# Modulation of the mixers: shift weights as halves, two tiles of activations each turn, first pieces of the recurrence split within the last turn

## The reference, cut to what matters

```python
s_lat, s_ctx = silu(c), silu(c_ctx)
m_lat = split(s_lat @ w_mod + b_mod, 6); m_ctx = split(s_ctx @ w_mod + b_mod, 6)
hx = rmsnorm(x, norm_mix) * (1 + m_lat[1]) + m_lat[0]
hc = rmsnorm(ctx, norm_mix) * (1 + m_ctx[1]) + m_ctx[0]
... = split_cols(hx @ w_in); ... = split_cols(hc @ w_in)
```

## Time and profile before

| | us |
|---|---|
| median of 3 runs | 3080.35 |
| profiled execution, its own time | 3083.66 |
| its span | 3081.8 |
| first product of the modulation starts | 13.22 |
| transposes of the tokens | 72.51 to 81.15 |
| last row of the modulation copied | 136.64 |
| first pieces of the recurrence | 147.86 to 172.42 |
| mean granted TensorE clock | 0.947 of full |

### The profile page before, as it was taken

How to read it: one execution, slowest core, us unless ns; L and a number is a source line. 1 busy time by engine, 2 the same in 40 slices (tenths; PEclk the granted TensorE clock), 3 DMA queues, 4 the chain that set the end, 5 groups by cost and what they waited for, 6 DMA issues and landing times.

```text
span 3081.8 us, 31629 instructions
## 1 busy us (share of the span) xinstructions
PE 2660.0 (86%) x11041; PEld 1807.1 (59%) x11041; DVE 1930.2 (63%) x2622; ACT 912.0 (30%) x1241; POOL 599.6 (19%) x580
## 2 busy tenths in 40 slices
PE   7899997999999999999999855969778876868777
PEld 3488875878776889998877723334333432323233
DVE  2389997443565868887555746555555665566645
ACT  1167775432544433333434100101111111101100
POOL 0000000000000000000000244434344434343333
PEclk9999998999999999999999977989989998989999
DMA  8633333542323968887555789999999999999998
GB/s 334 221 127 115 122 108 125 190 179 96 137 96 125 366 266 341 337 336 286 205 217 212 287 344 378 418 421 407 421 407 421 402 421 411 421 396 422 422 422 356
DMA packets 126508, 902.85 MB, mean 293 GB/s; under 512 B 14016, under 2 KB 15552, under 8 KB 17216
## 3 DMA queue, kind: packets, MB, share of 16 engines
q0 software_dynamic: 82944, 604.02, 47.7%
q1 hardware_dynamic: 38736, 278.94, 24.3%
q10 hardware_dynamic: 4720, 18.57, 1.6%
HBM read 899.33 MB, written 2.13 MB: 293 GB/s over the span
## 4 chain that ended last, share of the span: by engine, by line
PE 44%; DMA 29%; DVE 12%; issue 9%; ACT 3%; POOL 1%; DVEq 0%; ACTq 0%; POOLq 0%
DMA u<-in_peer_u,idx 27%; PE ps L445 9%; PE ps L488 7%; PE ps L490 7%; PE ps L489 7%; PE ps L765 5%; PE ps L503 3%; DVE u L1670 2%; DMA v<-in_peer_v,idx 2%; DVE wl L1148 2%; POOL v L1765 1%; PE ps L460 1%; ACT wh L827 1%; DVE ub L1232 1%; PE ps L642 1%
## 5 line engine op out<-in xcount | busy, mean ns | idle before, releaser
L765 PE MATMUL ps<-v,dg 128*128 128x512 f32 x1920 | 882.2, 616 | 188.5 <-DMA v<-in_peer_v,idx 92.7
L1670 DVE SCALAR_TENSOR_TENSOR u<-u,hN 128x2048 f32<-128x2048 f32 x256 | 586.5, 2292 | 495.8 <-DMA u<-in_peer_u,idx 484.4
L1148 DVE TENSOR_TENSOR wl<-w,wh 128x1024 fp32r<-128x1024 f32 x432 | 524.6, 1222 | 407.5 <-ACT wh L827 406.5
L765 PEld LDWEIGHTS ps<-v,dg 128*128 128x128 f32 x1920 | 370.7, 197 | 695.9 <-issue 538.0
L827 ACT ACTIVATE wh<-w 128x1024 fp32r<-128x1024 f32 x432 | 453.5, 1058 | 679.1 <-PE ps L490 411.8
L1755 POOL DMA_INDIRECT u<-in_peer_u,idx x256 | 270.1, 1055 | 856.0 <-DVE u L1670 447.5
L445 PE MATMUL ps<-both,wh 128*128 128x256 f32 x2048 | 372.4, 285 | 5.3 <-DVE y L1360 5.1
L1100 ACT ACTIVATE dg<-con,wt 128x128 f32<-128x128 f32 x240 | 93.0, 399 | 835.4 <-PE ps L765 830.2
L1765 POOL DMA_INDIRECT v<-in_peer_v,idx x256 | 295.3, 1154 | 198.0 <-PE ps L765 111.5
L445 PEld LDWEIGHTS ps<-both,wh 128*128 128x128 f32 x2048 | 321.0, 193 | 10.2 <-issue 9.0
L1747 POOL DMA_DIRECT2D mr<-in_wmod x64 | 34.0, 532 | 1397.7 <-DVE br_lo L1488 980.0
(11 more groups left out here) (240 smaller groups left out, 2807.3 us busy)
## 6 DMA issues: line engine op xcount, KB each, us to landing
w<-in_stream SPq DMA_DIRECT2D x260, 1024.0 KB, 4.8
mr<-in_wmod POOLq DMA_DIRECT2D x64, 1024.0 KB, 7.0
wg<-in_gates ACTq DMA_DIRECT2D x8, 512.0 KB, 3.4
wx<-in_stream SPq DMA_DIRECT2D x4, 1024.0 KB, 8.0
u<-in_peer_u,idx POOLq DMA_INDIRECT x256, 16.7
v<-in_peer_v,idx POOLq DMA_INDIRECT x256, 18.0
xs<-in_ctx ACTq DMA_DIRECT2D x1, 2048.0 KB, 17.3
xs<-in_x ACTq DMA_DIRECT2D x1, 2048.0 KB, 23.2
```

The lines of the kernel that those rows point to most:

```text
L765: last = mm(ps[:, b, :], dg[:, k % 4, :], V[n % NV][:, b * 512:(b + 1) * 512], start=(k == 0), stop=(k == TOPK - 1))
L1148: tt(wl[p % SPLITS][:, :, :], W[s][:, q * PIECE:(q + 1) * PIECE, :], wh[p % SPLITS][:, :, :].bitcast(F32), ALU.subtract)\
L1670: stt(U[n % NU][:, :], U[n % NU][:, :], 1.0, hN[:, t, :], ALU.mult, ALU.mult, accum_out=dot[:, t, k:k + 1])\
```

## The change: what it does

The rows of the shift and of the scale of the same 256 columns are made in one turn; there are eight turns c, and the stream is ordered so that each brings two halves of shift weights (`W[0]`, `W[1]`) and two of scale weights (`W[2]`, `W[3]`). The scale stays in f32. The shift weights are parted into `wh` and `wl` by ScalarE and VectorE, piece by piece, and multiplied in fp32r: `wh` against four columns (`sS`, the high and the low part of `sT`) and `wl` against two. After each turn its rows are copied, transposed (`rows_turn`) and made into columns (`mod_cols`) for two tiles. From turn 4 on, tiles are modulated inside the turns, two or four in each, the context side by ScalarE and the latent side by VectorE. The tokens' squares, their scaling and the copies of their transposes are shared out between ScalarE and VectorE, and between the splits; their DMAs are issued behind the first four splits. The tokens are transposed after turn 3. The first weight pieces of the recurrence are parted around the end of turn 7. Not shown: the new places of the small buffers, the lists of steps.

```diff
+        sS = sb("sS", R_S + 192, [P, KT, 4], F32R)
+        mrow = sb("mrow", R_S + 1216, [P, 2, 2 * CW])
...
+        MODS, MP = MOD_H // 4, 4
+        FREED = (3, 4, 7, 8)
+        mod_hi, mod_lo = sem("mod_hi"), sem("mod_lo")
+        xt_copied = [sem("xt_dve"), sem("xt_act")]
+        rows_copied, rows_turned = sem("rows_copied"), sem("rows_turned")
+        VM = Steps(sem("dve_mod"), ["b0", "b1", "s0", "s1"])
+        AH = Steps(sem("act_h"), ["vc", "hc", "hx"])
+        VV = Steps(sem("dve_v"), ["x"])
+        VH = Steps(sem("dve_h"), [f"lo_{w}" for w in "cx"])
+        SIDES = (("c", hc, 0, 1), ("x", hx, T, 0))
...
-            by_pe(1, LRU0 // RING + 1)
+            for i in range(1, LRU0 // RING + 1):
+                for s in (2, 0, 3, 1):
+                    if s < 2:
+                        sp.wait_ge(mod_lo, MP * (i - 1) + 2 * (s + 1))
+                    else:
+                        sp.wait_ge(piece_used, 8 * (i - 1) + 4 * s - 6)
+                    sp.dma_start(W[s][:, :, :], a_stream[i * RING + s].rearrange("p (k n) -> p k n", n=CW)).then_inc(arrived[s], 16)
...
+            def mod_turn(c):
+                b = 2 * (c % 2)
+                if c >= 2:
+                    pe.wait_ge(rows_copied, 2 * (c - 1))
+                for h_ in (0, 1):
+                    pe.wait_ge(arrived[2 + h_], 16 * (c + 1))
+                    for kk in range(HK):
+                        last = mm(ps[0:2, b + 1, 0:CW], sT[:, h_ * HK + kk, :], W[2 + h_][:, kk, :], start=(h_ == 0 and kk == 0),
+                                  stop=(h_ == 1 and kk == HK - 1), skip_group_check=True)
+                    last.then_inc(piece_used, 2)
+                    for p in (2 * h_, 2 * h_ + 1):
+                        m = MP * c + p
+                        pe.wait_ge(mod_lo, m + 1)
+                        for kk in range(PIECE):
+                            k = p * PIECE + kk
+                            mm(ps[0:4, b, 0:CW], sS[:, k, 0:4], wh[m % SPLITS][:, kk, :], start=(k == 0), stop=False, skip_group_check=True)
+                            last = mm(ps[0:2, b, 0:CW], sS[:, k, 0:2], wl[m % SPLITS][:, kk, :], start=False,
+                                      stop=(k == KT - 1), skip_group_check=True)
+                        last.then_inc(piece_used, 1)
+                    if h_ == 0 and c >= 4:
+                        rows_turn(c - 1)
+            def rows_turn(c):
+                pe.wait_ge(rows_copied, 2 * (c + 1))
+                if c:
+                    pe.wait_ge(*VM.at(c - 1, "s0"))
+                for i in range(2):
+                    nc.tensor.transpose(ps[:, 4, 4 * i:4 * i + 4], mrow[0:4, c % 2, i * P:(i + 1) * P], ident[0:4, 0:4])
+                for i in range(2):
+                    last = nc.tensor.transpose(ps[:, 4, 8 + 2 * i:10 + 2 * i], mrow[0:2, c % 2, CW + i * P:CW + (i + 1) * P], ident[0:2, 0:2])
+                last.then_inc(rows_turned, 1)
+            def first_piece(p):
+                pe.wait_ge(*VH.at((p + 1) * PIECE - 1, "lo_x"))
+                proj_both(LRU0, 0, 0, 0, part=(p,))
+            pe.wait_ge(*V0_.at(0, "sl"))
+            for c in range(2):
+                mod_turn(c)
             pe.wait_ge(par_in, 32)
+            rows_turn(0)
+            mod_turn(2)
+            rows_turn(1)
+            mod_turn(3)
             for k in range(KT):
                 if k == 0:
+                    pe.wait_ge(*VM.at(1, "s0"))
+                    pe.wait_ge(*A0.at(0, "xn1"))
                     pe.wait_ge(*V0_.at(0, "xn3"))
                 if k >= 4:
-                    pe.wait_ge(*V0_.at(0, f"xT{k - 4}"))
+                    pe.wait_ge(xt_copied[k % 2], (k - 4) // 2 + 1)
                 for t in range(4):
                     last = nc.tensor.transpose(ps[:, 4 + k % 4, t * P:(t + 1) * P], xs[:, t, k * P:(k + 1) * P], ident)
                 last.then_inc(*P0.inc(f"xT{k}"))
-            mod_turns(MOD_H // 8, MOD_H // 4)
-            pe.wait_ge(*VM.at(MOD_H // 4 - 1, "m1"))
+            pe.wait_ge(xt_copied[0], KT // 2)
+            rows_turn(2)
+            for c in range(4, MODS):
+                mod_turn(c)
+            first_piece(0)
+            rows_turn(MODS - 1)
+            for p in range(1, 4):
+                first_piece(p)
...
+            act.wait_ge(par_in, 32)
+            fn(sig0[:, :], pc("c", 0, 2 * KT), ACT.Sigmoid).then_inc(*A0.inc("sig"))
+            def mod_split(m):
+                c, p = divmod(m, MP)
+                act.wait_ge(arrived[p // 2], 16 * (c + 1))
+                if c:
+                    act.wait_ge(piece_used, 8 * (c - 1) + FREED[p])
+                fn(wh[m % SPLITS][:, :, :], W[p // 2][:, p % 2 * PIECE:(p % 2 + 1) * PIECE, :], ACT.Copy).then_inc(mod_hi, 1)
+            def tiles(c):
+                act.wait_ge(*VM.at(c, "s1"))
+                for k in (2 * c, 2 * c + 1):
+                    for w, to, at, v in SIDES:
+                        x, scale, bias = xT[:, k, at:at + T], mcol[:, KT + k, v:v + 1], mcol[:, k, v:v + 1]
+                        if w == "c":
+                            fn(x, x, ACT.Identity, scale=scale, bias=bias).then_inc(*AH.inc("vc"))
+                            act.wait_ge(*AH.at(k, "vc"))
+                        else:
+                            act.wait_ge(*VV.at(k, "x"))
+                        fn(to[0][:, k, :], x, ACT.Copy).then_inc(*AH.inc("h" + w))
+            for m in range(4):
+                mod_split(m)
             act.dma_start(xs[:, 0:2, :], a_ctx.rearrange("(t p) d -> p t d", p=P)).then_inc(xs_in, 16)
             act.dma_start(xs[:, 2:4, :], a_x.rearrange("(t p) d -> p t d", p=P)).then_inc(xs_in, 16)
-            act.wait_ge(par_in, 32)
-            fn(sig0[:, :], pc("c", 0, 2 * KT), ACT.Sigmoid).then_inc(*A0.inc("sig"))
             act.wait_ge(*V0_.at(0, "abs"))
             fn(lm[2][:, :], lm[1][:, :], ACT.Exp, scale=-1.0).then_inc(*A0.inc("ez"))
+            for m in range(4, 8):
+                mod_split(m)
             act.wait_ge(xs_in, 32)
             for i in range(4):
                 if i:
                     act.wait_ge(*A0.at(0, f"ss{i - 1}"))
                 fn(junk[:, :], xs[:, i, :], ACT.Square, accum_out=ssq[:, i:i + 1]).then_inc(*A0.inc(f"ss{i}"))
+                mod_split(8 + i)
             act.wait_ge(*A0.at(0, "ss3"))
             act.wait_ge(*V0_.at(0, "eps"))
             fn(rin0[:, :], ssq[:, :], ACT.Sqrt, scale=1.0 / D, bias=tiny[:, 1:2]).then_inc(*A0.inc("rt"))
+            mod_split(12)
+            act.wait_ge(*V0_.at(0, "rin"))
+            for i in (0, 1):
+                fn(xs[:, i, :], xs[:, i, :], ACT.Copy, scale=rin0[:, i:i + 1]).then_inc(*A0.inc(f"xn{i}"))
+                mod_split(13 + i)
+            mod_split(15)
+            for k in range(1, KT, 2):
+                act.wait_ge(*P0.at(0, f"xT{k}"))
+                fn(xT[:, k, :], ps[:, 4 + k % 4, :], ACT.Copy).then_inc(xt_copied[1], 1)
             def split(first, turn, per, p, slots=None):
@@ -827,12 +903,17 @@
                 fn(wh[p % SPLITS][:, :, :], W[s][:, q * PIECE:(q + 1) * PIECE, :], ACT.Copy).then_inc(hi_done, 1)
-            for k in range(KT):
-                for w, to, at in (("c", hc, 0), ("x", hx, T)):
-                    act.wait_ge(*VH.at(0, f"{w}{k}"))
-                    if k % PIECE == 0 and w == "c":
-                        split(LRU0, 0, 0, k // PIECE)
-                    fn(to[0][:, k, :], xT[:, k, at:at + T], ACT.Copy).then_inc(*AH.inc(f"{w}{k}"))
+            for c in range(4, MODS):
+                for p in range(4):
+                    mod_split(MP * c + p)
+                for i in {4: (0, 1), 5: (2, 3), 6: (4, 5)}.get(c, ()):
+                    tiles(i)
+            split(LRU0, 0, 0, 0)
+            split(LRU0, 0, 0, 1)
+            tiles(MODS - 2)
+            split(LRU0, 0, 0, 2)
+            tiles(MODS - 1)
+            split(LRU0, 0, 0, 3)
...
+            dve.wait_ge(*V0_.at(0, "st"))
+            def mod_low(m):
+                c, p = divmod(m, MP)
+                dve.wait_ge(mod_hi, m + 1)
+                tt(wl[m % SPLITS][:, :, :], W[p // 2][:, p % 2 * PIECE:(p % 2 + 1) * PIECE, :], wh[m % SPLITS][:, :, :].bitcast(F32), ALU.subtract)\
+                    .then_inc(mod_lo, 1)
+            def mod_rows(c):
+                if c >= 2:
+                    dve.wait_ge(rows_turned, c - 1)
+                dve.wait_ge(piece_used, 8 * c + 8)
+                nc.vector.tensor_copy(mrow[0:4, c % 2, 0:CW], ps[0:4, 2 * (c % 2), 0:CW]).then_inc(rows_copied, 1)
+                nc.vector.tensor_copy(mrow[0:2, c % 2, CW:2 * CW], ps[0:2, 2 * (c % 2) + 1, 0:CW]).then_inc(rows_copied, 1)
+            def mod_cols(c):
+                dve.wait_ge(rows_turned, c + 1)
+                got = ps[:, 4, 0:8].rearrange("p (b v) -> p b v", v=4)
+                shift, scale = mcol[:, 2 * c:2 * c + 2, :], mcol[:, KT + 2 * c:KT + 2 * c + 2, :]
+                wide_ = lambda x: x.unsqueeze(2).to_broadcast([P, 2, 2])
```

(94 more changed lines are left out.)

18 lines of the change are left out of this document (1 added, 17 removed).

## The result

The changed kernel takes 3053.2 us, the median of 4 runs (3051.26 to 3056.05), beside 3080.83 (3078.01 to 3081.86) of the kernel before. The ratio is 0.9913, with an interval of 0.9895 to 0.9930: 27 us, or 0.9%, faster. The forecast was 3052. Its range of 3040 to 3066 holds the time.

A forecast was written before the change was run, and what follows sets the result against it. TensorE, busy 2660.0 of 3081.8 us, and a serial joint were to bound the first stage. fp32r 24.6, joint some 16, transposes 1.5, less about 14 for waits, save 28.5: 3080.35 becomes 3052, range 3040 to 3066.

The forecast's parts named there:

- fp32r at 0.120: Shift matmuls in the modulation: 0.120 us each, bounds 0.113 and 0.216; over eight turns 24.6 us go.
- Rival C: Shift matmuls: fp32r with few columns held still costs 0.216, a turn 13.8; 16 us saved, 3064; chance 0.06.
- Turn 1 hangs on transfers: Modulation turn 1: tokens' DMAs, issued at 16.7, fall into the reloads; last half lands at 38, turn ends at 41.5.
- Turn 2 hangs on ScalarE's squares: Modulation turn 2: four splits stand between four squares of 1.905 on ScalarE; last split at 51.8, end 54.
- Turns 4 to 7: Modulation after the transposes: turns 4, 5 and 7 take 10.75 and 0.3 us each, turn 6 12.6; end at 119.2.
- A: Modulation turns: all waits hidden, only TensorE counts, 10.75 a turn; 39 us saved, 3041; chance 0.08.
- B: Weight loads of the turns: they stay at 262 to 300 GB/s, 14 us a turn; 20 saved, 3060; chance 0.08.
- D: Modulation turns: hand-overs pace them, turns 4 to 7 take 13.5, turns 1 to 3 five more; 14 saved, 3066; chance 0.09.
- The weighing of the 358 GB/s: Turns' loads: at this HBM limit 11.7 us a turn, some 8 us more over eight; left out of the sum.
- The split of the saving: Head of the kernel: 24.6 us from fp32r, some 16 from the joint, 1.5 from transposes; about 14 given to waits.
- Rival E: Modulation: after short gaps TensorE's clock stays at 1.2 GHz, its 86 us of work takes twice that; 3125; chance 0.04.
- Rival F: Behind 172 us: saved time is given back, as ring or gate loads can't start early; 3078 to 3082; chance 0.03.

The follow-up runs named there:

- C: The changed kernel itself, against the kernel before: 3053.2 us, ratio 0.9913; profiled again in three later executions beside the follow-up runs.
- half loads: The changed kernel with half of the bytes in each weight load of turns 1 to 7, values left wrong: median 3052.2 us.
- Late orders: Changed kernel with VectorE's order, late reloads (turns 5 to 7, last four) and the recurrence's first two split waits edited: 3048.23 and 3049.81 us.

## Why the prediction was right

Its sum, forecast beside C's first profile: turn 0 ends at 26 (25.7), turn 1 at 41.5 (39.6), turn 2 at 54 (53.0), turn 3 at 65.6 (64.2), turn 4 starts at 73.6 (72.05), turn 7 ends at 119.2 (120.1), the first piece starts at 121.7 (122.17), the pieces end at 143.9 (146.35; 144.40, 144.58 and 149.73 in C's other profiles). The head was to give 28.5 us; C's four profiles have 26.1, 28.0, 27.8 and 22.7, so the 1.2 us between the forecast of 3052 and the median is closer than one profile can tell. The path was the right one, and so was its price for the whole, though terms of its sum were off and cancelled. The parts:

- **fp32r at 0.120**: measured 0.114, inside the bounds. Rival C is out. TensorE's busy time fell by 23.6 us in the head, all terms together, against 24.6 for this one.
- **Turn 1 hangs on transfers**: it does (1.5 us for the load, 1.0 for the low part of W[0]), but the step about the tokens' DMAs was wrong: they were issued at 12.19, not 16.7, as soon as the constants had landed (12.15) and ahead of the four splits written before them, whose loads had landed at 5.5 and 8.5. So what is said ahead of the prediction, that nothing but TensorE's weight loads passes anything, does not hold for a DMA's issue. The last load of turn 1 landed at 34.6 instead of 38, TensorE did not wait for it, and the turn ended 1.9 us earlier than forecast.
- **Turn 2 hangs on ScalarE's squares**: in part. TensorE waited 1.7 us before its second piece, for a split behind a square; but ScalarE had itself waited 2.5 us for the load of W[0], landed at 41.06, and with half loads the wait is gone though the squares are the same.
- **Turns 4 to 7**: forecast 45.6 us, measured 48.0. The end of turn 7 came out near (119.2, 120.1) because turn 4 had begun 1.5 us early. The forecast had ScalarE held by its tiles and put a loss of 1.7 in turn 6; the waits are 1.0 in turn 6 and 0.6 in turn 7, and they need late loads as well. Without them a turn still takes 11.3 us (from the second f32 half of turn 4 to that of turn 5 in the half loads, 74.42 to 85.70) and not the forecast's 11.05. At 12.0 us a turn rivals A (10.75), B (14) and D (13.5) are out for these turns. The weighing of the 358 GB/s that the prediction took from the Trainium skill left the loads out altogether, and that was too quick. In C the streams moved, over the last three turns,

```profile
84.00:126.00 42.00, 38.18 (x215) 19.00 (x215) 32.86 (x72) 26.19 (x45) 0.00 (x0) 0.96 0.93 356
```

  while 10 to 30 us has 405 and 424. The Trainium skill ("DMA: Bandwidth & Descriptors", Specifications) has about 358 GB/s for one core; the trace passes it for these 20 us, and on the profile's page 15 of the last 16 slices, each 76 us long and with gathers among the loads, have 379 to 422. So 358 was no ceiling of this core in these stretches, and that 356 is near it proves nothing; what slows the loads of the turns (the pauses between reloads that wait for their buffers, or something else) no run separates. The 8 us that this rule would have cost is near the 6.1 that half loads gave, but of those only 2.0 lie in turns 4 to 7. Rival B (20 saved) was the nearest of the others in mechanism, too dear in size.
- **The gap before the first piece**: forecast 2.5 us from VectorE's queue, measured 2.1 (1.0 to 3.5 in the others). In C's first profile the load of W[0] ended the wait, landed at 119.7 and split by 120.8, with VectorE free at 120.4; in its second and third VectorE's queue ended it: two paths nearly level, of which the forecast saw one. Late orders had to move both, and the split's own wait.
- **The split of the saving**: this sentence fails. "Some 16 from the joint" did not even follow from the turn-by-turn list, which has 24.7 us from turn 7's end to the pieces' end against 35.8 before, 11. The shift in f32 shows the joint by itself: 13.3 us. In C it gives 9.6 (26.3 us from turn 7's end to the pieces' end), since there the first piece waits and the clock dips, and the other 16.4 lie ahead of turn 7's end. What an edit is worth depends on what is already there: the turns in f32 save 13.3 and fp32r on top of them 12.7; fp32r in turns with the tiles behind them saves 20.7 and the move of the tiles 5.4. Both ways sum to 26.07. The overestimated joint (16, measured 9.6) and the overestimated waits (14, where TensorE's waits inside the turns and before the first piece sum to 8) cancelled, and that was luck.
- **The clock** was forecast at 1.0 for the first piece. In C's first profile it dipped:

```profile
120.00:130.00 10.00, 7.90 (x30) 6.17 (x30) 4.94 (x12) 5.20 (x9) 0.00 (x0) 0.83 0.74 301
```

  and the piece took 7.28 us instead of the 5.46 to 5.73 of the profiles without a dip. Rival E's mechanism exists, at 1.8 us where E had 86 us of work take twice as long.
- **Rival F** (given back later) is out: the rest of the span is no longer than before.

## What to carry to other kernels

When an engine's work is made cheaper by giving its neighbours new work, list the gain twice: by the engine's own busy time in the whole change, and by undoing the edit alone; here 23.6 and 12.7 us. A turn in which the engine, its helpers and the loads each need nearly the whole period hangs on late loads and on the work that stands behind them together. Here the order of the reloads gave 2.4 us (49.0 to 46.5 from turn 4's start to the first piece), but cost 2 us of waits for W[3] where it was changed in turns 1 and 3 too, and the exact count that a split waits for 0.6. A difference of 2 us at a joint between two single profiles is worth nothing until the same kernel has been profiled again: C's ends lie 5.3 us apart.

## What the runs showed of the hardware that was not expected

- A short standstill can be followed by the lower level of the clock. Ahead of the first piece TensorE stood still for 0.6, 1.0, 1.2 and 1.6 us without a dip, and for 2.1, 2.1, 3.5 and 3.5 us with one (granted 0.5 for a while, the 1.2 GHz level). A wait of 2.5 us in turn 1 of late orders was followed by one too, waits of 1.0 to 1.8 in the turns of C by none. The length alone does not decide it: in the kernel before TensorE stood still for 2.2 us ahead of the transposes, and the clock was granted in full from 72 to 84 us (first stretch below). In C's first profile the dip cost 1.8 us.

```profile
72.00:76.00 4.00, 3.49 (x31) 3.31 (x32) 3.84 (x8) 0.00 (x0) 0.00 (x0) 1.00 0.62 252
```

- ScalarE's queue issued a DMA written behind four ACTIVATEs at 12.19 us, 0.12 us before the first of them began.
- The same load in the same kernel landed up to 3.7 us apart between executions (69.8 and 73.4; start of the transposes 64.3 to 65.6 in C), which sets a floor for what a profile can tell in a stage that hangs on transfers.
